# Identity matmuls ahead of the token transposes and of the first projection; token tiles transposed one after the other, sums of squares later

## The reference, cut to what matters

```python
def rmsnorm(x, w):
    xf = x.astype(jnp.float32)
    y = xf * lax.rsqrt(jnp.mean(xf * xf, axis=-1, keepdims=True) + RMS_EPS)
    return (y * w.astype(jnp.float32)).astype(x.dtype)

    xn = rmsnorm(x, ln1_w)
    z = xn @ w_in            # (tokens, 1024) @ (1024, 3592)
    ...                      # block-sparse attention and mLSTM on parts of z
    x = x + mix @ w_out
    hn = rmsnorm(x, ln2_w)
    x = x + jnp.square(jax.nn.relu(hn @ w_up)) @ w_down
```

## Time and profile before

| | |
|---|---|
| median of 3 runs | 711.54 us (710.98 to 711.67) |
| the profiled execution, its own time | 711.88 us |
| its span, first to last instruction | 710.1 us |
| TensorE matmul busy | 690.1 us, 97% of the span |
| VectorE, ScalarE, GpSimdE busy | 451.7, 296.0, 313.3 us |
| mean granted TensorE clock | 0.994 |

### The profile page before, as it was taken

The page is one execution under the profiler, slowest core; times in us unless marked ns, Lnnn a source line. Parts: engine busy times, 40 slices in busy tenths (PEclk is TensorE's granted clock), DMA queues, the critical chain, the costliest instruction groups (busy, mean ns, idle before and its releaser), DMA issues.

```text
span 710.1 us, 15199 instructions
## 1 busy us (share of the span) xinstructions
PE 690.1 (97%) x5563; PEld 643.6 (91%) x5563; DVE 451.7 (64%) x894; ACT 296.0 (42%) x568; POOL 313.3 (44%) x229
## 2 busy tenths in 40 slices
PE   6989899999999999999999999999999999999996
PEld 6988798969678777899999999999999999999996
DVE  4497988895342537637698695856748567575133
ACT  6252644545453222326645545235343344334222
POOL 6227998923223244244327807144080532606531
PEclk9999899999999999999999999999999999999999
DMA  7727898844664858842302333313133231423103
GB/s 245 235 83 204 265 294 246 255 140 122 212 196 153 279 162 292 152 149 65 115 1 66 120 114 120 120 60 119 59 118 118 85 95 60 159 78 119 60 1 121
DMA packets 88633, 100.41 MB, mean 141 GB/s; under 512 B 5374, under 2 KB 64338, under 8 KB 88570
## 3 DMA queue, kind: packets, MB, share of 16 engines
q1 hardware_dynamic: 74566, 92.91, 42.1%
q10 hardware_dynamic: 14004, 6.67, 3.9%
HBM read 92.92 MB, written 6.64 MB: 140 GB/s over the span
## 4 chain that ended last, share of the span: by engine, by line
PE 79%; DVE 10%; issue 3%; ACT 3%; POOL 3%; DMA 1%; SPq 0%; DVEq 0%; ACTq 0%; POOLq 0%
PE acc L898 7%; PE acc L899 6%; PE acc L900 6%; PE acc L1402 5%; PE acc L1401 5%; PE acc L1403 5%; PE scr L1402 3%; PE scr L1403 3%; PE scr L1401 3%; PE scr L1368 3%; PE scr L1367 3%; PE scr L1369 3%; PE acc L1367 3%; PE acc L1368 3%; PE acc L1369 3%
## 5 line engine op out<-in xcount | busy, mean ns | idle before, releaser
L898 PE MATMUL acc<-act_hi,w_hi 128*128 128x256 f32 (+1 forms) x416 | 123.1, 296 | 1.1 <-DVE zT L2479 1.1
L899 PE MATMUL acc<-act_lo,w_hi 128*128 128x256 f32 (+1 forms) x416 | 118.3, 284 | 0.0
L900 PE MATMUL acc<-act_hi,w_lo 128*128 128x256 f32 (+1 forms) x416 | 118.0, 284 | 0.0
L1997 POOL TENSOR_TENSOR h_lo<-relu,h_hi 128x520 fp32r<-128x520 f32 x32 | 44.2, 1384 | 165.0 <-ACT h_hi L1788 164.6
L1952 POOL TENSOR_TENSOR prod<-kv,Qb 128x1024 f32<-128x1024 f32 x32 | 85.9, 2715 | 34.4 <-DVE S L2181 18.8
L1487 POOL TENSOR_TENSOR w_lo<-raw,w_hi 128x1024 fp32r<-128x1024 f32 x20 | 47.7, 2384 | 97.6 <-ACT w_hi L1480 97.6
L898 PEld LDWEIGHTS acc<-act_hi,w_hi 128*128 128x128 f32 x416 | 79.3, 191 | 7.7 <-issue 5.3
L899 PEld LDWEIGHTS acc<-act_lo,w_hi 128*128 128x128 f32 x416 | 79.4, 191 | 0.0
L900 PEld LDWEIGHTS acc<-act_hi,w_lo 128*128 128x128 f32 x416 | 79.2, 190 | 0.0
L2498 DVE TENSOR_TENSOR xT<-acc,xT 128x260 f32<-128x260 f32 x64 | 26.7, 426 | 48.4 <-PE acc L1403 48.4
L2479 DVE TENSOR_TENSOR zT<-acc,rstd 128x264 f32<-128x264 f32 (+1 forms) x56 | 23.5, 423 | 50.4 <-PE acc L900 47.8
(11 more groups left out here) (422 smaller groups left out, 2311.9 us busy)
## 6 DMA issues: line engine op xcount, KB each, us to landing
kv<-in_cache_k_dram SPq DMA_DIRECT2D x64, 256.0 KB, 3.5
kv<-in_cache_v_dram SPq DMA_DIRECT2D x64, 256.0 KB, 3.1
raw<-in_w_up_dram SPq DMA_DIRECT2D x16, 1024.0 KB, 5.5
raw_d<-in_w_down_dram SPq DMA_DIRECT2D x12, 1024.0 KB, 5.1
raw<-in_w_in_dram SPq DMA_DIRECT2D x14, 512.0 KB, 5.7
raw<-in_w_in_dram SPq DMA_DIRECT2D x7, 1024.0 KB, 7.5
x_tok<-in_x_prompt_dram SPq DMA_DIRECT2D x8, 512.0 KB, 5.7
raw<-in_w_out_dram SPq DMA_DIRECT2D x4, 1024.0 KB, 7.7
```

The source lines that it names most:

```text
L898: pe.matmul(out, w_hi[:, slot, k, :], hi[k][:, cols], start=(n == 0), stop=False)
L899: pe.matmul(out, w_hi[:, slot, k, :], lo[k][:, cols], start=False, stop=False)
L900: mm = pe.matmul(out, w_lo[:, slot, k, :], hi[k][:, cols], start=False, stop=(n == KT - 1))
L1997: pool.tensor_tensor(h_lo[:, t, :], relu2[:, t % 2, :], h_hi[:, t, :].bitcast(F32), ALU.subtract).then_inc(s_hs_lo, 1)
```

## The change: what it does

The identity's diagonal is written right behind its fill, with a semaphore for itself; the two other small tables have their own (`even_ok`), for which only the later job "own" waits. TensorE then runs six plain matmuls of the identity with itself into an unused PSUM bank, transposes the sample tokens, all of tile 2, `ln1_w`, all of tile 3, and runs another six identity matmuls before slot 0. The sample tokens and `ln1_w` go to banks of `acc`, out of the list of jobs. On ScalarE the sum of squares of tile 2 leaves its place ahead of the split; both sums now stand behind `w_hi` of weight tiles 0 and 1. On GpSimdE `w_lo` of weight tile 1 comes ahead of the powers. VectorE waits for the identity alone.

```diff
+WARM = 6
-    job("param", 0)
-    job("xs", 0)
+            def early_tile(c, i):
+                pe.wait_ge(x_in[i], 16)
+                for n in range(4):
+                    out = bank("x1", n) if c else open_job(pe, "x1", n)
+                    for j in (2 * n, 2 * n + 1):
+                        col = (j % 2) * SPLIT_TOK + c * P
+                        mm = pe.transpose(out[:, col:col + P], x_tok[:, i, j * P:(j + 1) * P], ident[:, :])
+                    if c:
+                        done(mm)
+            def keep_busy():
+                for _ in range(WARM):
+                    pe.matmul(acc[:, 3, 0:P], ident[:, :], ident[:, :], start=True, stop=True)
-            pe.wait_ge(s_ident_ok, 3)
-            out = open_job(pe, "param", 0)
-            pe.wait_ge(s_ln1_in, 16)
-            done(pe.transpose(out[:, 0:KT], ln1_rows[:, :], ident[0:KT, 0:KT]))
-            out = open_job(pe, "xs", 0)
+            pe.wait_ge(s_ident_ok, 1)
+            keep_busy()
             pe.wait_ge(x_in[NT], 16)
             for j in range(KT):
-                mm = pe.transpose(out[:, j * NS:(j + 1) * NS], x_s[:, j * P:(j + 1) * P], ident[0:NS, 0:NS])
-            done(mm)
-            for n in range(4):
-                x_to_cols(("x1", n), n, (2, 3))
+                mm = pe.transpose(acc[:, 2, j * NS:(j + 1) * NS], x_s[:, j * P:(j + 1) * P], ident[0:NS, 0:NS])
+            mm.then_inc(s_xs_up, 1)
+            early_tile(0, 2)
+            pe.wait_ge(s_ln1_in, 16)
+            pe.transpose(acc[:, 1, 0:KT], ln1_rows[:, :], ident[0:KT, 0:KT]).then_inc(s_ln1_up, 1)
+            early_tile(1, 3)
+            keep_busy()
 ...
                 elif name == "own":
                     pe.wait_ge(s_samp_dve, 2)
+                    pe.wait_ge(s_even_ok, 2)
 ...
-            out = full(act, "param", 0)
-            free(act.activation(par[:, 0:KT], out[:, 0:KT], ACT.Copy), "param", 0)
-            square_sum(2)
-            out = full(act, "xs", 0)
-            free(act.activation(xn_s[:, :, :].rearrange("p j b -> p (j b)"), out[:, 0:KT * NS], ACT.Copy), "xs", 0)
-            evacuated(act, "param", 0)
+            act.wait_ge(s_xs_up, 1)
+            act.activation(xn_s[:, :, :].rearrange("p j b -> p (j b)"), acc[:, 2, 0:KT * NS], ACT.Copy)\
+               .then_inc(s_xs_copied, 1)
+            act.wait_ge(s_ln1_up, 1)
+            act.activation(par[:, 0:KT], acc[:, 1, 0:KT], ACT.Copy).then_inc(s_ln1_ok, 1)
+            act.wait_ge(s_ln1_ok, 1)
             for n in range(4):
                 x_hi(("x1", n), n, 1)
                 if n == 1:
                     split(0)
+            split(1)
+            square_sum(2)
             square_sum(3)
-            split(1)
             split(2)
 ...
             pool.memset(ident[:, :], 0.0).then_inc(s_pool_chain, 1)
+            pool.wait_ge(s_pool_chain, 1)
+            pool.affine_select(out=ident[:, :], in_=ident[:, :], compare_op=ALU.not_equal, fill=1.0, base=0,
+                               pattern=[[-1, P]], channel_multiplier=1).then_inc(s_ident_ok, 1)
 ...
             weight_lo(pool, 0, 0, 0)
+            weight_lo(pool, 1, 1, 0)
             pool.wait_ge(s_x_ms_ok, 2)
             rsqrt(rs[:, 2:NT], P, 2).then_inc(s_x_rs_ok, 1)
             rsqrt(rs[0:NS, NT:NT + 1], NS, 1).then_inc(s_x_rs_ok, 1)
-            weight_lo(pool, 1, 1, 0)
             weight_lo(pool, 2, 2, 1)
 ...
-            dve.wait_ge(s_ident_ok, 3)
+            dve.wait_ge(s_ident_ok, 1)
 ...
-            evacuated(dve, "param", 0)
+            dve.wait_ge(s_ln1_ok, 1)
 ...
-            evacuated(dve, "xs", 0)
+            dve.wait_ge(s_xs_copied, 1)
```

More of the change, by code:

```diff
@@ L570, in build @@
         s_ident_ok = sem("ident_ok")
+        s_even_ok = sem("even_ok")
+        s_ln1_up = sem("ln1_up")
+        s_ln1_ok = sem("ln1_ok")
+        s_xs_up = sem("xs_up")
+        s_xs_copied = sem("xs_copied")
         s_causal_ok = sem("causal_ok")
@@ L1913, in _ @@
             pool.wait_ge(s_pool_chain, 5)
-            pool.affine_select(out=ident[:, :], in_=ident[:, :], compare_op=ALU.not_equal, fill=1.0, base=0,
-                               pattern=[[-1, P]], channel_multiplier=1).then_inc(s_ident_ok, 1)
             pool.affine_select(out=causal[:, SEQ - P:SEQ], in_=causal[:, SEQ - P:SEQ], compare_op=ALU.is_ge,
@@ L1920, in _ @@
             pool.affine_select(out=even[:, 0:1], in_=even[:, 0:1], compare_op=ALU.is_ge, fill=1.0, base=-64,
-                               pattern=[[1, 1]], channel_multiplier=1).then_inc(s_ident_ok, 1)
+                               pattern=[[1, 1]], channel_multiplier=1).then_inc(s_even_ok, 1)
             pool.affine_select(out=even[:, 1:2], in_=even[:, 1:2], compare_op=ALU.is_ge, fill=1.0, base=63,
-                               pattern=[[1, 1]], channel_multiplier=-1).then_inc(s_ident_ok, 1)
+                               pattern=[[1, 1]], channel_multiplier=-1).then_inc(s_even_ok, 1)
             for rows_split in (qs_split, M_split):
```

## The result

The changed kernel takes 721.78 us (median of 5 runs, 721.62 to 723.23), the kernel before 711.41 (5 runs, 710.98 to 711.67): ratio 1.0151, 95% interval 1.014 to 1.0162. It is 1.5% slower, 10.4 us, where 711.0 was forecast. The profiled execution of the changed kernel took 721.62 with a span of 719.9; before it was 711.88 with 710.1. So the two traces differ by 9.8 us.

What follows compares the result with a forecast made beforehand. TensorE bounds the kernel, with slot 0 waiting for ScalarE. ScalarE's gain of 0.75 us becomes 0.55 at slot 3 and passes whole: 711.88 - 0.55 = 711.3 profiled, 711.0 median; 8-in-10 range 709.5 to 712.5.

Steps and rivals of the forecast that it cites:

- the price of the identity matmuls: TensorE's beginning: first six take 2.6 us, hidden by the wait for loads; second six hidden ahead of slot 0, 0.9 spare.
- After it: From 22 us to the end: the 0.55 us gained by slot 3 passes whole to the total time.
- Rival (3): Before slot 0: identity matmuls themselves late at the low clock, a loss of 1.8 to 2.4 us, 713.6; chance 0.08.
- ScalarE's start: Beginning: ScalarE starts at 6.7 instead of 7.45 us, a gain of 0.75; bounds 6.5 to 7.5.
- the upper bound: Beginning, low clock throughout: tile 2 and `ln1_w` done at 6.8, two transposes of tile 3, ScalarE starts at 7.5 us.
- `w_hi` of weight tile 2 at 15.14: ScalarE's beginning: it waits for its load until 15.14, hiding the moved sums of squares, done at 14.4, with 0.7 spare.
- The K pages: SyncE: first K page issued at 16.38, second sum of squares done at 14.4, so 2 us to spare.
- TensorE waits for `act_lo` in slot 0: Sign in the changed profile: slot 0 starts at 9.1 to 9.5 us and still contains a wait for `act_lo`.
- the wait of the rstd broadcast for its bank near 18: After slot 1: a new TensorE wait for a bank VectorE frees at 18.1; broadcast starts at 18.2 instead of 18.81.
- Rival (2): Until slot 0: the clock stays low or falls again, gain 0 to loss 0.4 us, 711.7; chance 0.25.
- Rival (4): TensorE at 73 to 80 us: changed timing spares the low clock, worth up to 3.3 us, 708.2; chance 0.19.

Runs made afterwards that it cites:

- e10: Changed kernel with five instead of six identity matmuls in each place and transposes of tiles 2 and 3 alternating behind `ln1_w`: 710.94 us, ratio 0.9989.
- e2: Changed kernel with five instead of six identity matmuls in each of the two places: 711.60 us, ratio 1.0007.
- e4: Changed kernel without any identity matmul, all else as in it: 712.12 us, ratio 1.0013.
- e5: Kernel before with 41 more TensorE instructions (83 useless waits) at its beginning: 711.43 us (one run).

## Why the prediction was wrong

*The step that failed* is the price of the identity matmuls, together with "After it. [...] the 0.55 pass whole to the end (bounds: nothing, or with later alignments some 0.8 either way)". They were priced as time beside the loads at the beginning, and that was right: 10 or 16 of them cost 0 to 0.2%, within what can be told. Left out was that 12 matmuls are 48 instructions of a stream that is loaded in blocks and has a loop 6500 instructions later. The missing term measured +9.8 (9.4 to 10.5 over the bodies of 1548), or 0 by the place in the block, and it stood in none of the cases. Rival (3) had the right sign by the wrong mechanism.

What the profile before could have told: a row for q8 with 39 loads, a second iteration without a single one, and loads just before the branch that place the loop's start. With 6 x 256 + 12 in the body, 11 of 256 starts are bad by theory A1; the edit moved the start by 45 from about 202, to 247. It could be counted, though the row for q8 alone doesn't say how many blocks are held: without these runs it was a risk of a few per cent.

*ScalarE's start* was off too: 8.30, where 6.7 was taken and 6.5 to 7.5 were the bounds. I took a gain from "by then TensorE has worked for over 3 us", but the transposes of both tiles ran 0.22 apart (1.97 for eight). So the chain of the upper bound held ("4.9 + 1.8 + 0.1 = 6.8, [...] 7.5"), and was 0.8 short: the identity matmuls began at 1.60 and not 1.4 and took 2.93 and not 2.6, which with the sample tokens' 1.02 makes 5.5 for 4.9, and tile 2 and `ln1_w` took another 0.2 more. With tile 2 whole ahead of tile 3, ScalarE had nothing to start on meanwhile; e10, alternating, has it at 6.97.

*Right:* `w_hi` of weight tile 2 at 15.14 was to cover the moved squares, which it did to within 0.28 (15.42), in spite of a start 1.6 later than reckoned. The K pages went out at 16.56 (16.38 in the earlier trace rows). TensorE waits for `act_lo` in slot 0, as before. *Not seen:* the wait of the rstd broadcast for its bank near 18: slot 1 itself ended so late that it came at 19.58 without one. Rival (2), a beginning that gains nothing, is what the beginning did: with good starts the kernels end at 711.6 to 712.1 (e2 to e4). Rival (4) named the stretch at 73 to 80 rightly as what later timing can spare, and its bound of 3.3 was five times too large: VectorE has no gap there, and 0.5 to 0.7 at the loop's start is all that went with it.

## What to carry to other kernels

A loop on TensorE whose body touches seven or eight blocks of 256 instructions, by where it starts, has a price that hangs on that start. So an edit anywhere ahead of it on the same engine, a useless wait included, can cost 10 us. Bodies far from this length weren't run. Look at the instruction queue's loads in the window of the second iteration: if they appear where the other kernel has none, pad or trim a few instructions before judging the edit. And time each edit of a beginning at two paddings: a delay of 0.8 us at 20 us was gone by 414 us here.

## What the hardware showed

- Seven blocks of 16 KB, a body of 1548 instructions, are kept over a taken branch: 86.13 us of TensorE without a load (before, e2, e4, e5). Eight are not, and nine loads come again. The Trainium skill, "Runtime: NRT & Kernel Launch", section "Instruction fetch mechanics", says that a taken branch whose target isn't in the current window of two pages forces a fetch that the engine must wait for. The gaps of 6.4 to 7.9 us agree; the window of two pages does not, by the iterations without a load. The same section states 2048 instructions of memory for TensorE, which is eight blocks of 256. That fits better: seven blocks of the body and one loaded ahead make eight, and with eight of the body there would be nine. How far ahead a block is loaded is inferred, as is that whole blocks are held: from nine starts and three body lengths, not read from an address.
- The stall costs about half as much again through the clock: granted 0.50, 1.2 GHz, for 10.24 us, which begin 2.8 us after the matmuls stop (505.19 to 515.43 in the changed kernel).
- Transposes alone brought the high level. In e4 nothing but transposes precedes slot 0, which begins 0.12 apart (first three rows). It is 0.22 apart from 12.0 on, behind two idle stretches of 1.47 and 0.45 us; the last two rows give the granted clock, 1.00 in 10 to 11 and 0.50 in 12 to 13:

```profile
10.03 0.36 PE L921 MATMUL acc<-act_hi,w_hi 128*128 128x264 f32 x1 [1.47 <-ACT w_hi L1501]
10.23 0.28 PE L922 MATMUL acc<-act_lo,w_hi 128*128 128x264 f32 x1
10.35 0.29 PE L921 MATMUL acc<-act_hi,w_hi 128*128 128x264 f32 x1
...
11.70 0.50 PE L921 MATMUL acc<-act_hi,w_hi 128*128 128x264 f32 x1 [0.45 <-DVE act_lo L2103]
...
12.22 0.42 PE L921 MATMUL acc<-act_hi,w_hi 128*128 128x264 f32 x1
12.44 0.42 PE L922 MATMUL acc<-act_lo,w_hi 128*128 128x264 f32 x1
```
```profile
10.00:11.00 1.00, 0.97 (x8) 1.00 (x8) 0.27 (x2) 1.00 (x4) 0.98 (x1) 1.00 1.02 417
...
12.00:13.00 1.00, 1.00 (x6) 1.00 (x6) 0.47 (x3) 1.00 (x2) 0.99 (x2) 0.50 1.10 356
```

  In the kernel before the transposes run from 5.21 to 9.91 and the fast spacing comes only in slot 0, near 11.6; in e4 they run from 3.22 to 8.57. The Trainium skill, "TensorE: Matmul & The Clock Gate", Part 4 (PE-mode transpose), which the prediction cited, holds that transposes don't count as activity that raises the clock; e4 does not bear that out.
